# The first ffn_up chunk multiplies x before it is normalised

## What is computed

```
yx = ... @ w_out                                   # 256 x 1024
x  = x + mx[:, :, 2] * yx
h2 = modulate(rmsnorm(x, norm2_g), shift, scale)   # x * rstd(token) * g * (1 + scale) + shift
x  = x + mx[:, :, 5] * conv_ffn(h2, ffn_up, ...)
# conv_ffn: z = h2 @ ffn_up (1024 x 5632), a 3x3 depthwise convolution of z on a 4 x 64 grid,
# silu(first half) * second half, @ ffn_down (2816 x 1024)
```

## Time and profile before

| | us |
|---|---|
| three runs | 732.5, 725.23, 732.14 (median 732.14) |
| profiled execution, whole | 733.28 |
| its span in the trace | 731.4 |
| PE busy | 716.5 (98%) |
| DVE busy | 492.2 (67%) |
| POOL busy | 390.5 (53%) |
| ACT busy | 358.3 (49%) |

### The profile page before, as it was taken

The page is one execution under the profiler, slowest core; times in us unless marked ns, Lnnn a source line. Parts: engine busy times, 40 slices in busy tenths (PEclk is TensorE's granted clock), DMA queues, the critical chain, the costliest instruction groups (busy, mean ns, idle before and its releaser), DMA issues.

```text
span 731.4 us, 14173 instructions
## 1 busy us (share of the span) xinstructions
PE 716.5 (98%) x5848; PEld 694.0 (95%) x5848; DVE 492.2 (67%) x906; ACT 358.3 (49%) x459; POOL 390.5 (53%) x219
## 2 busy tenths in 40 slices
PE   6899999999999989999999999999999999999998
PEld 3798889999999989999999999999999999999998
DVE  3886897669536369877777775467946766666663
ACT  6688135245435456555555457435664434334331
POOL 0778553556548958878887887766877000000000
PEclk9999999999999989999999999999999999999999
DMA  8994888337534637555544555334344655655611
GB/s 358 419 413 167 345 310 312 127 116 257 210 115 169 205 112 293 177 192 202 184 173 175 187 205 184 120 122 163 125 165 161 216 204 176 225 182 174 221 58 58
DMA packets 21233, 145.84 MB, mean 199 GB/s; under 512 B 2481, under 2 KB 3249, under 8 KB 3890
## 3 DMA queue, kind: packets, MB, share of 16 engines
q1 hardware_dynamic: 21024, 144.87, 54.6%
q10 hardware_dynamic: 146, 0.07, 0.0%
HBM read 143.88 MB, written 1.05 MB: 198 GB/s over the span
## 4 chain that ended last, share of the span: by engine, by line
PE 94%; DVE 3%; issue 1%; ACT 1%; DMA 0%; DVEq 0%; ACTq 0%
PE bank L1445 24%; PE bank L1447 24%; PE bank L1446 24%; PE bank L1464 5%; PE CP L1446 2%; PE CP L1447 2%; PE CP L1445 2%; PE bank L1556 2%; PE bank L1489 1%; DVE ada_s L919 1%; DVE SPARE L919 1%; PE bank L1504 1%; PE CP L1478 1%; PE bank L1818 1%; PE bank L1471 0%
## 5 line engine op out<-in xcount | busy, mean ns | idle before, releaser
L472 POOL TENSOR_TENSOR wlo<-raw,whi 128x512 fp32r<-128x512 f32 (+1 forms) x185 | 354.7, 1947 | 144.4 <-ACT whi L490 143.6
L490 ACT ACTIVATE whi<-raw 128x2048 fp32r<-128x2048 f32 x100 | 191.0, 1911 | 54.8 <-DMA raw<-in_w_in 28.4
L1212 DVE SCALAR_TENSOR_TENSOR Y<-bank,vec,Y 128x189 f32<-128x189 f32 (+2 forms) x352 | 122.9, 421 | 41.3 <-ACT Y L745 41.3
L1445 PE MATMUL bank<-H2h,whi 128*128 128x256 f32 x352 | 100.4, 285 | 1.7 <-DVE H2l L1187 1.7
L1446 PE MATMUL bank<-H2l,whi 128*128 128x256 f32 x352 | 100.1, 284 | 0.0
L1447 PE MATMUL bank<-H2h,wlo 128*128 128x256 f32 x352 | 100.1, 284 | 0.0
L1445 PE MATMUL bank<-H1h,whi 128*128 128x256 f32 (+1 forms) x288 | 89.8, 312 | 2.7 <-DVE H1l L938 1.9
L1447 PE MATMUL bank<-H1h,wlo 128*128 128x256 f32 (+1 forms) x288 | 88.1, 306 | 0.0
L1446 PE MATMUL bank<-H1l,whi 128*128 128x256 f32 (+1 forms) x288 | 88.0, 306 | 0.0
L871 DVE TENSOR_TENSOR wlo<-raw,whi 128x2048 fp32r<-128x2048 f32 x29 | 66.4, 2292 | 31.6 <-ACT whi L490 31.6
L1445 PE MATMUL bank<-H4h,whi 128*128 128x256 f32 x256 | 70.9, 277 | 0.0
(11 more groups left out here) (329 smaller groups left out, 1920.7 us busy)
## 6 DMA issues: line engine op xcount, KB each, us to landing
raw<-in_w_mlp SPq DMA_DIRECT2D x32, 1024.0 KB, 4.9
raw<-in_w_in SPq DMA_DIRECT2D x30, 1024.0 KB, 6.1
raw<-in_ffn_up SPq DMA_DIRECT2D x22, 1024.0 KB, 4.9
raw<-in_ada_hi SPq DMA_DIRECT2D x16, 1024.0 KB, 5.2
...
```

The lines of the kernel that those rows point to most:

```text
L472: m = e.tensor_tensor(l[:, a:a + step], r[:, a:a + step], h[:, a:a + step].bitcast(F32), ALU.subtract)
L490: e.activation(whi[q % NHI][:, :], raw[n % NRAW][:, :], ACT.Copy).then_inc(s["w_hi"], 1)
L1212: e.scalar_tensor_tensor(o[:, r0:r1, c0:c1], z[:, r0 + dr:r1 + dr, c0 + dc:c1 + dc], cw[:, f, tap:tap + 1], o[:, r0:r1, c0:c1], ALU.mult, ...
L1445: e.matmul(out, h[:, col:col + P], xh, start=first, stop=False, skip_group_check=True)
```

## The change

Chunk 0 of ffn_up is multiplied by `x * A2` without the row: `UXh` and `UXl` hold the high and low parts, 8 tiles of 256 columns, and behind them the shift as column 257 (and once more as 258). The sums go to banks 4 and 5, one for each output tile. The row is applied afterwards: DVE takes the sum of the shift column out of PSUM (SHC), multiplies the 256 token columns by the row in place, and ACT adds SHC in place. Chunks 1 to 21 use H2h and H2l as before. Chunk 1 goes to bank 6. The matmuls on UXh and UXl stand in three groups around the sums of squares and the row. The row is copied from PSUM to SBUF (RR) by ACT before DVE uses it. ACT makes whi of ffn_up chunk 2 ahead of the root, and that of chunk 3 behind the H2h tiles. ffn_down chunk 0 moves from behind ffn_up chunk 5 to behind chunk 4. `ends["ffn_up", 0]` now frees the memory for the bias load.

```diff
-        if i >= 5 and i % 2:
+        if i == 4:
+            plan.append(("ffn_down", 0, 2048))
+        if i >= 7 and i % 2:
             plan.append(("ffn_down", (i - 5) // 2, 2048))
...
+    def up(i, j):
+        if i == 0:
+            return bank[4 + j][:, 0:T]
+        return (bank[6] if i == 1 else product("ffn_up", i))[:, j * T:(j + 1) * T]
...
+        def raw_high(k):
+            e.activation(UXh[:, k, 0:T], XR[:, k, :], ACT.Identity, scale=A2[:, k:k + 1]).then_inc(s["h2_hi"], 1)
+
         warm(ACT.Sqrt)
+        e.wait_ge(s["mods"], 5)
+        e.activation(UXh[:, :, T:T + 2], MODX[:, 8:16].unsqueeze(2).to_broadcast([P, KT, 2]),
+                     ACT.Copy).then_inc(s["h2_hi"], 1)
         for i in range(4):
             high(turn["w_out", i] + 2)
             for f, n in ([(2 * i, 2)] if i < 3 else [(6, 1), (7, 1)]):
                 e.wait_ge(s["x1"], f + n)
                 e.activation(SQ1[:, f:f + n, :], XR[:, f:f + n, :], ACT.Square).then_inc(s["sq1"], 1)
+                if i < 3:
+                    raw_high(f)
+                    raw_high(f + 1)
+        high(turn["ffn_up", 2])
+        raw_high(6)
         e.wait_ge(s["col_x"], 1)
         root(misc_bank["col1"], 2, D, 0, "rms_x")
+        raw_high(7)
         warm(ACT.Silu)
+        e.wait_ge(s["row_x"], 1)
+        e.activation(RR[:, :], bank[misc_bank["row1"]][:, 0:T], ACT.Copy).then_inc(s["rr_done"], 1)
         ...
+        high(turn["ffn_up", 3])
...
+                    e.wait_ge(s["h2_mul"], 12)
+                    for j in range(2):
+                        z = up(0, j)
+                        e.activation(z, z, ACT.Identity, bias=SHC[:, j:j + 1]).then_inc(s["mid"], 1)
+                    e.wait_ge(s["mid"], 2)
...
+        def raw_low_tile(k):
+            e.wait_ge(s["x1"], k + 1)
+            e.wait_ge(s["h2_hi"], k + 2)
+            e.scalar_tensor_tensor(UXl[:, k, 0:T], XR[:, k, :], A2[:, k:k + 1], UXh[:, k, 0:T].bitcast(F32),
+                                   ALU.mult, ALU.subtract).then_inc(s["h2_lo"], 1)
+
+        project("w_out", 0, "x1", SQ1, "sq1", "sq1_sum", raw_low)
+        raw_low_tile(6)
         reciprocal(2, 0, ("rms_x", 1), "rstd_x")
+        raw_low_tile(7)
+        e.wait_ge(s["rr_done"], 1)
...
+        def first_chunk():
+            e.wait_ge(s["gemm"], ends["ffn_up", 0])
+            for j in range(2):
+                e.tensor_copy(SHC[:, j:j + 1], bank[4 + j][:, T:T + 1]).then_inc(s["h2_mul"], 1)
+            for j in range(2):
+                e.tensor_tensor(up(0, j), up(0, j), RR[:, :], ALU.mult).then_inc(s["h2_mul"], 1)
...
+        raw_products((0, 1))
         e.wait_ge(s["sq1_sum"], 2)
         square_columns(bs, SQ1, 0, 2)
         ...
         m.then_inc(s["col_x"], 1)
+        raw_products((2, 3, 4))
         b = misc("row1")
         e.wait_ge(s["rstd_x"], 1)
         rows(b, [wide(0), wide(1)], "row_x")
+        raw_products((5, 6, 7)).then_inc(s["gemm"], 1)
...
-        for i in range(24):
-            if i == 1:
-                rows(group("ffn_up", 1), [wide(0), wide(1)], None)
+        rows(bank[7], [wide(0), wide(1)], None)
+        for i in range(1, 24):
             if i < 22:
-                pair("ffn_up", i, H2h, H2l, ready=h2_ready if i == 0 else None)
-            if i >= 5 and i % 2:
+                pair("ffn_up", i, H2h, H2l, ready=h2_ready if i == 1 else None)
+            if i == 4:
+                e.wait_ge(s["conv"], 32)
+                contract("ffn_down", 0, AH, AL, NA, "a_hi", "a_lo", 1, 21)
```

More of the change, by code:

```diff
@@ L113, in product_tables @@
             e = [(x, 2 * i + 2)] if i < 3 else [(x, 7), (x, 8)]
-        elif name == "ffn_up":
+        elif name == "ffn_up" and i >= 2:
             e = [("conv", 16 * i + 16)]
@@ L220, in build @@
     G2 = keep("G2", [P, KT, 2])
+    SHC = keep("SHC", [P, 2])
     GS = keep("GS", [P, KT])
@@ L300, in build @@
     H2l = area("H2l", [P, KT, T], 32, F32R)
+    UXh = area("UXh", [P, KT, 320], 72, F32R)
+    UXl = area("UXl", [P, KT, 320], 84, F32R)
     BI = area("BI", [P, 8, 384], 72)
@@ L440, in sync @@
             if n == place["ffn_up", 2] + 5:
-                e.wait_ge(s["gemm"], ends["w_out", 3])
+                e.wait_ge(s["gemm"], ends["ffn_up", 0])
                 e.dma_start(BI[:, :, :], io["bias"]).then_inc(s["late_in"], 16)
@@ L738, in scalar @@
                 high(turn["ffn_up", i] + 2)
-                b = product("ffn_up", i)
-                e.wait_ge(s["gemm"], ends["ffn_up", i])
+                if i:
+                    e.wait_ge(s["gemm"], ends["ffn_up", i])
+                else:
+                    e.wait_ge(s["h2_mul"], 12)
[3 more added lines that the diff above has]
+                    e.wait_ge(s["mid"], 2)
                 if i >= 4:
@@ L744, in scalar @@
                     f = i + 22 * j
-                    e.activation(Y[i % 4][:, j, :], b[:, j * T:(j + 1) * T], ACT.Identity, bias=v("conv_b", f, 1),
+                    e.activation(Y[i % 4][:, j, :], up(i, j), ACT.Identity, bias=v("conv_b", f, 1),
                                  scale=cw[:, f, 4:5]).then_inc(s["mid"], 1)
@@ L760, in scalar @@
                 warm(ACT.Sqrt)
-            if i >= 5 and i % 2:
-                high(turn["ffn_down", (i - 5) // 2] + 2)
         high(turn["ffn_down", 10] + 2)
@@ L1177, in project, with raw_low @@
                 lower((6 + j,))
-        project("w_out", 0, "x1", SQ1, "sq1", "sq1_sum", lambda ks: None)
+        e.wait_ge(s["h2_hi"], 1)
+        e.wait_ge(s["mods"], 5)
+        e.tensor_tensor(UXl[:, :, T:T + 2], MODX[:, 8:16].unsqueeze(2).to_broadcast([P, KT, 2]),
+                        UXh[:, :, T:T + 2].bitcast(F32), ALU.subtract).then_inc(s["h2_lo"], 1)
+        def raw_low(ks):
+            for k in ks:
+                if k < 6:
+                    raw_low_tile(k)
+        def raw_low_tile(k):
[5 more added lines that the diff above has]
+        raw_low_tile(6)
         reciprocal(2, 0, ("rms_x", 1), "rstd_x")
-        e.wait_ge(s["row_x"], 1)
-        e.wait_ge(s["mods"], 5)
+        raw_low_tile(7)
+        e.wait_ge(s["rr_done"], 1)
         e.wait_ge(s["x1"], 8)
         def h2_low(k):
-            e.wait_ge(s["h2_hi"], k + 1)
+            e.wait_ge(s["h2_hi"], KT + 1 + k + 1)
             e.scalar_tensor_tensor(H2l[:, k, :], TMP1[:, k, :], MODX[:, 8 + k:9 + k], H2h[:, k, :].bitcast(F32),
@@ L1262, in project_in @@
             if i == 0:
[L1263 removed]
+                e.wait_ge(s["rr_done"], 3)
             at_ = 2 * slot2[i]
@@ L1721, in tensor, with raw_products @@
         pair("w_out", 3, MGh, MGl, apart=True)
+        def raw_products(ks):
+            h, l = weights("ffn_up", 0)
+            for k in ks:
+                e.wait_ge(s["h2_hi"], k + 2)
+                e.wait_ge(s["h2_lo"], k + 2)
+                for j in range(2):
+                    m = mm3(bank[4 + j][:, 0:T + 2], h, l, (j * KT + k) * P, UXh[:, k, 0:T + 2], UXl[:, k, 0:T + 2],
+                            k == 0, k == KT - 1)
+            return m
+        for free in acc1_free[0:2]:
+            e.wait_ge(s[free[0]], free[1])
+        raw_products((0, 1))
         e.wait_ge(s["sq1_sum"], 2)
@@ L1754, in contract @@
                     m.then_inc(s["gemm"], 1)
-        for free in acc1_free:
+        for free in acc1_free[2:]:
             e.wait_ge(s[free[0]], free[1])
-        for i in range(24):
-            if i == 1:
-                rows(group("ffn_up", 1), [wide(0), wide(1)], None)
+        rows(bank[7], [wide(0), wide(1)], None)
+        for i in range(1, 24):
             if i < 22:
-                pair("ffn_up", i, H2h, H2l, ready=h2_ready if i == 0 else None)
-            if i >= 5 and i % 2:
+                pair("ffn_up", i, H2h, H2l, ready=h2_ready if i == 1 else None)
+            if i == 4:
+                e.wait_ge(s["conv"], 32)
+                contract("ffn_down", 0, AH, AL, NA, "a_hi", "a_lo", 1, 21)
+            if i >= 7 and i % 2:
                 contract("ffn_down", (i - 5) // 2, AH, AL, NA, "a_hi", "a_lo", 1, 21)
```

20 lines of the change are left out of this document (10 added, 10 removed).

## The result

The changed kernel takes **734.72 us** in the median of 14 launches, the kernel before **732.21** in the median of 14 on the same chip. The ratio is 1.0073, with a 95% interval of 1.0046 to 1.010: slower, but by less than the 1% that was to be told from no change. The forecast was 739.0 with a range of 733.5 to 743.

A forecast was written before the change was run, and what follows sets the result against it. TensorE was taken as the bound, holding 94% of the chain of waits. Late UXl tiles, row and convolution delay the weights, so chunk 6 starts 6.9 us later: 732.14 + 6.9 = 739.0 us, range 733.5 to 743.

The forecast's parts named there:

- The rule named there: DVE instruction with two SBUF inputs contends with GpSimd instruction reading SBUF; loser blocked throughout; tile 5 waits 4.45 us.
- turns that don't matter: UXl tiles run beside POOL without waiting; chunk 6's wlo at 300.9, -2.1, 730.0 us; chance 0.11.
- tile 5 first: UXl tile 5 precedes POOL's ffn_up chunk 1 instruction, or waits are short; +2.7, 734.8 us; chance 0.15.
- more waits or a loop that doesn't catch up: Another UXl tile behind a 4.5 us instruction, or loop not catching up; +10 to +12, 743 us; chance 0.10.
- Step 4: TensorE on ffn_up chunks 0 and 1: half clock after idling, chunk 1 ends at 280.8, 4 to 6 us late.
- the sum's last term: Chunk 6 of ffn_up starts at 309.9 instead of 303.01; its +6.9 us is carried whole to the end.
- second rival: UXl tile 5 ahead of POOL's ffn_up chunk 1 instruction, or short waits; +2.7, 734.8 us; chance 0.15.
- third rival: More waits of UXl tiles than counted, or loop not catching up; +10 to +12, 743 us; chance 0.10.
- The class: Whole kernel's time within about 1% (7.3 us) of the kernel before, not told from no change; chance 0.61.

The follow-up runs named there:

- the first experiment: Changed kernel with POOL's wlo of ffn_up chunks 0, 1 and 2 in four 512-column instructions instead of one of 2048; 733.97 us median, ratio 1.002 to the kernel before.
- the root-first variant: Changed kernel with ACT's whi of ffn_up chunk 2 moved behind the root and UXh tile 7; 739.42 us in one launch.

## Why the prediction was right, and where not

**Right in its steps up to chunk 6, but for one.** w_out chunk 2 waited 1.04 us (forecast 1.1). The last x came at 262.17 (262.3), through a UXl tile of over 4 us and its neighbour behind POOL's 2048-column instructions. TMP started at 271.20 (270.9), the last H2l ended at 278.14 (277.85), the convolution came at 281.22 (281.1), gate 0 ended at 289.92 (289.9) and the gates were 6.08 apart (6.09). The three weights behind them were ready at 297.72, 303.83 and 309.92 (297.7, 303.8, 309.9), chunk 6 started at 310.03 (309.9). The rule named there (the Trainium skill, SBUF — State Buffer, section "Who interferes with whom") agrees with the 4.40 us tile and the first experiment: the wait lasts until the other's instruction is through. None of the rivals occurred: turns that don't matter (-2.1), tile 5 first (+2.7), more waits or a loop that doesn't catch up (+10 to +12).

**Off on the way, at no cost.** TensorE was through with its work ahead of ffn_down chunk 0 at 296.07, not 297.75, and waited 1.87 instead of nothing. Most of that is the clock. Step 4 has it back "6.2 us after the row's start, as before", so near 276; but before, the row started at 257.81 and the clock was back at 266.4, 8.6 later, and 6.2 is only the length of a window in the earlier trace rows. After the change it was back at 272.7, 3.2 behind the row's start at 269.55, and chunk 1 ended at 279.58, not 280.8. The rest is the pace: chunks 2 to 4 took 5.44 us each, not 5.65. The end is set by the weight, so this changed nothing.

**Wrong: the sum's last term**, "733.28 + 6.9 = 740.2". It took the rest of the loop as unchanged, that is 0.1177 us a matmul in both kernels, from one window of one execution. The rows show 0.1178 before and 0.1133 after from 310.8 on, worth 5.5 us, so the profiled execution ends 1.39 later, not 6.9. Four launches of the changed kernel took 739.6 to 740.2, which is the 740.2 of the sum. None of them has a profile. That they kept the slower pace is read from the size of the step alone, and from the root-first variant, whose profile shows the slower pace from 309.2 on at 739.42 us. In the same way no launch of the kernel before in its lower group has a profile; 1557 x 0.0045 = 7.0 is about the 6.7 between its groups. The three times of before (725.23 beside two at 732) had the two groups in them already; a median over them was taken where the question was what a 7 us step between launches of one kernel is.

**The class and the range.** "Within 1%" came true (1.0073), at a chance of 0.61, and 734.72 lies in the range of 733.5 to 743. Both were luck in part. The median is 4.3 us below the forecast and outside the 736.5 to 741.5 that had a chance of 0.64. It lies on the second rival's number (734.8), by another mechanism than that rival's. Group against group the change costs 7.7 to 8.8 us, which is over the 7.3 of the class. In the chances, a third of 0.64 and the third rival's 0.10 make 0.31, not 0.36; the working doesn't say where the other 0.05 comes from.
